# mLSTM outputs of heads 0, 2 and 3 as three products of high and low parts

## The reference

```python
def step(carry, xs):                       # one chunk of 64 steps, all heads at once
    C, n, m = carry
    qc, kc, vc, ic, fc = xs
    b = jnp.cumsum(fc, axis=-1)
    dmat = jnp.where(causal, b[..., :, None] - b[..., None, :] + ic[..., None, :], -jnp.inf)
    inter = b + m[..., None]
    m_row = jnp.maximum(inter, dmat.max(-1))
    w_intra = jnp.exp(dmat - m_row[..., None])
    w_inter = jnp.exp(inter - m_row)
    s = jnp.einsum('bhid,bhjd->bhij', qc, kc) * w_intra
    num = jnp.einsum('bhij,bhjd->bhid', s, vc) + w_inter[..., None] * jnp.einsum('bhvk,bhik->bhiv', C, qc)
    den = s.sum(-1) + w_inter * jnp.einsum('bhk,bhik->bhi', n, qc)
    h = num / jnp.maximum(jnp.abs(den), jnp.exp(-m_row))[..., None]
    ...
mu = hh.mean(-1, keepdims=True)
var = jnp.mean(jnp.square(hh - mu), axis=-1, keepdims=True)
hn = ((hh - mu) * lax.rsqrt(var + LN_EPS)).transpose(0, 2, 1, 3).reshape(B, S, ML_INNER)
hn = hn.astype(h.dtype) * ln_w
return ((hn + skip * x_conv) * jax.nn.silu(z)) @ w_out
```

## Time and profile before

| | |
|---|---|
| median of 3 runs | 1936.8 us |
| profiled execution | 1933.06 us |
| its span | 1931.1 us |
| mean granted clock of TensorE | 0.989 |
| share of the span: TensorE, VectorE, ScalarE, GpSimd | 96%, 57%, 36%, 11% |
| first and last start of the output matmuls (line 1095) | 249.1 and 380.3 us |

### The profile page before, as it was taken

One profiled execution on the slowest core, in us unless ns is written; L12 is line 12 of the kernel. 1 busy time (PEld: TensorE's weight loads), 2 busy tenths in 40 slices (PEclk: granted clock), 3 DMA queues, 4 the chain that ended last, 5 costly groups with the idle time before them and its releaser, 6 DMA issues. The chain is left out here.

```text
span 1931.1 us, 35675 instructions
## 1 busy us (share of the span) xinstructions
PE 1851.7 (96%) x15284; PEld 1484.9 (77%) x15284; DVE 1097.6 (57%) x1648; ACT 693.0 (36%) x1154; POOL 221.5 (11%) x221
## 2 busy tenths in 40 slices
PE   8999999999999899999999899999899999999996
PEld 7887757688887666778888568878878888888875
DVE  4664354563256777444366887777465635354534
ACT  4325332341223787442212473423233322122342
POOL 4210011140002000210021340000001000000011
PEclk9999999999999999999999999999999999999998
DMA  5334323152224010124321100002042322322121
GB/s 187 115 109 142 130 77 116 44 209 99 69 69 141 3 45 2 67 92 141 125 100 55 47 2 4 4 3 69 4 175 90 107 98 90 106 92 105 55 98 44
DMA packets 42379, 160.73 MB, mean 83 GB/s; under 512 B 4976, under 2 KB 14192, under 8 KB 27632
## 3 DMA queue, kind: packets, MB, share of 16 engines
q1 hardware_dynamic: 28016, 143.78, 21.7%
q10 hardware_dynamic: 14208, 14.68, 2.1%
HBM read 140.36 MB, written 16.78 MB: 81 GB/s over the span
## 5 line engine op out<-in xcount | busy, mean ns | idle before, releaser
L257 DVE TENSOR_TENSOR wlo<-raw,whi 128x2048 fp32r<-128x2048 f32 (+2 forms) x113 | 251.4, 2225 | 183.9 <-ACT whi L248 183.6
L248 ACT ACTIVATE whi<-raw 128x2048 fp32r<-128x2048 f32 (+2 forms) x113 | 209.0, 1850 | 317.9 <-PE ps L283 161.4
L281 PE MATMUL ps<-act_hi,whi 128*128 128x512 f32 x616 | 243.6, 395 | 0.0
L301 PE MATMUL ps<-act_lo,whi 128*128 128x512 f32 x632 | 242.0, 392 | 0.0
L283 PE MATMUL ps<-act_hi,wlo 128*128 128x512 f32 x616 | 240.8, 391 | 0.0
L282 PE MATMUL ps<-act_lo,whi 128*128 128x512 f32 x616 | 240.7, 391 | 0.0
L300 PE MATMUL ps<-act_hi,whi 128*128 128x512 f32 x592 | 235.5, 398 | 0.0
L305 PE MATMUL ps<-act_hi,wlo 128*128 128x512 f32 x632 | 156.5, 389 | 0.0
L301 PEld LDWEIGHTS ps<-act_lo,whi 128*128 128x128 f32 x632 | 119.7, 189 | 25.6 <-issue 1.2
L305 PEld LDWEIGHTS ps<-act_hi,wlo 128*128 128x128 f32 x632 | 118.6, 188 | 24.6
L300 PEld LDWEIGHTS ps<-act_hi,whi 128*128 128x128 f32 x592 | 111.1, 188 | 32.2 <-issue 8.1
(11 more groups left out here) (520 smaller groups left out, 3362.0 us busy)
## 6 DMA issues: line engine op xcount, KB each, us to landing
raw<-stream_in SPq DMA_DIRECT2D x107, 1024.0 KB, 4.9
v_scratch<-v_out ACTq DMA_DIRECT2D x16, 256.0 KB, 3.3
z_scratch<-zt ACTq DMA_DIRECT2D x16, 256.0 KB, 2.9
mlh_v<-v_scratch SPq DMA_DIRECT2D x4, 1024.0 KB, 4.8
mlh_z<-z_scratch SPq DMA_DIRECT2D x16, 256.0 KB, 2.6
cmp_w<-cmp_w_in SPq DMA_DIRECT2D x2, 2048.0 KB, 11.3
z_scratch<-in_zt ACTq DMA_DIRECT2D x16, 256.0 KB, 2.2
mix_g<-z_scratch SPq DMA_DIRECT2D x16, 256.0 KB, 6.9
```

The costliest lines, as they stand in the source:

```text
L248: act.activation(k.whi[b % 2][:, 0:n], k.raw[b % RAW_SLOTS][:, 0:n], ACT.Copy).then_inc(k.hi_done, 1)
L257: dve.tensor_tensor(k.wlo[b % 2][:, 0:n], k.raw[b % RAW_SLOTS][:, 0:n], k.whi[b % 2][:, 0:n].bitcast(F32), ALU.subtract).then_inc(k.lo_don ...
L281: pe.matmul(bank, hi, x_hi, start=(x == 0), stop=False)
L301: pe.matmul(bank, hi, x_lo, start=False, stop=False)
```

## The change

Heads 0, 2 and 3 (`SPLIT`) get `split_outputs` in place of `outputs`; head 1 stays as it was. For a split head `v` and `st` are each divided in a high part (`v_hi`, `st_hi`, fp32r copies by ScalarE) and a low part (`v_lo` by GpSimd, `st_lo` by VectorE). A pair (i, j) then is five fp32r matmuls: three of 128x512 and two with two columns of ones (`one`) for the row sum. The parts are laid in places that are used up: `v_lo` in place of `v`, `st_lo` in place of `st`, `st_hi` over the keys whose blocks the scores have read, `v_hi` over `hn` for head 0 and over `xconv` of heads 0 and 1 for heads 2 and 3. The row sums move to every second column of their bank. The line numbers below are those of the kernel before.

```diff
--- before.py
+++ after.py
@@ -962,6 +962,11 @@
     wexp = k.region("mlh_wexp", [P, 2, S], F32, 64)
     z = k.region("mlh_z", [P, 2, S], F32, 68)
     y = k.region("mlh_y", [P, 2, S], F32, 74)
+    SPLIT = [0, 2, 3]
+    v_lo = k.region("mlh_v_lo", [P, TT, S], F32R, 32)
+    v_hi = {h: k.region(f"mlh_v_hi{h}", [P, TT, S], F32R, at) for h, at in zip(SPLIT, (40, 0, 8))}
+    st_hi, st_lo = k.region("mlh_st_hi", [P, TT, S], F32R, 48), k.region("mlh_st_lo", [P, TT, S], F32R, 56)
+    one = k.region("mlh_one", [P, 2], F32R, 72)
     sc = k.small
     den, adn, r, sd, scale, shift = (sc[:, 32 + 4 * i:36 + 4 * i] for i in range(6))
     stats = sc[:, 64:64 + 24].rearrange("p (t s) -> p t s", s=6)
@@ -971,7 +976,7 @@
           "v_landed", "k_mm", "k_act", "k_dve", "nm_mm",
           "sc_mm", "wexp_raw", "wexp_done", "st_done", "h_mm", "hn_done", "hn_dve",
           "tr_mm", "y_read", "y_done", "y_hi", "y_lo", "step", "r2v_done",
-          "sd_done", "scale_done")}
+          "sd_done", "scale_done", "v_hi", "v_lo", "st_hi", "st_lo", "one")}
     zl = [k.sem(f"mlh_z_landed{i}") for i in range(2)]
     LAST = ML_HEADS - 1
 
@@ -985,6 +990,13 @@
 
     def add_bank(n):
         return (4 + n) % 8
+
+    def diagonal(j):
+
+        return st_hi[:, 0:TT - j, j * P:(j + 1) * P]
+
+    def blocks(j):
+        return st[:, j, j * P:S].rearrange("p (i q) -> p i q", q=P)
 
     with k.joined() as block:
         @block.sync
@@ -1034,8 +1046,15 @@
                 pool.tensor_tensor(k.act_lo[:, a, :], y[:, u % 2, :], k.act_hi[:, a, :].bitcast(F32), ALU.subtract) \
                     .then_inc(s["y_lo"], 1)
 
+            def values_low(h):
+                pool.wait_ge(s["v_hi"], SPLIT.index(h) + 1)
+                for j in range(TT):
+                    last = pool.tensor_tensor(v_lo[:, j, :], v[:, j, :], v_hi[h][:, j, :].bitcast(F32), ALU.subtract)
+                last.then_inc(s["v_lo"], 1)
+
             for j in range(TT):
                 triangle(0, j)
+            values_low(0)
             for h in range(ML_HEADS):
                 for c in range(TT):
                     if h < LAST and c == 0:
@@ -1044,6 +1063,8 @@
                         triangle(h + 1, 2)
                     if h < LAST and c == 1:
                         triangle(h + 1, 3)
+                    if c == 2 and h + 1 in SPLIT:
+                        values_low(h + 1)
                     low(h, c)
             norm.gather(pool)
 
@@ -1093,7 +1114,28 @@
                     for j in range(i + 1):
                         lhs = st[:, j, i * P:(i + 1) * P]
                         pe.matmul(k.ps[:, i, :], lhs, v[:, j, :], start=(j == 0), stop=(j == i))
-                        last = pe.matmul(k.ps[:, 7, i:i + 1], lhs, k.const("ones")[:, 0:1], start=(j == 0), stop=(j == i))
+                        last = pe.matmul(k.ps[:, 7, 2 * i:2 * i + 1], lhs, k.const("ones")[:, 0:1], start=(j == 0), stop=(j == i))
+                    last.then_inc(s["h_mm"], 1)
+
+            def split_outputs(h):
+                x = SPLIT.index(h)
+                pe.wait_ge(s["one"], 1)
+                pe.wait_ge(s["v_lo"], x + 1)
+                for i in range(TT):
+                    pe.wait_ge(s["st_lo"], TT * x + i + 1)
+                    if h:
+                        pe.wait_ge(s["y_read"], TT * (h - 1) + i + 1)
+                        pe.wait_ge(s["r2v_done"], h)
+                    if h == 2:
+                        pe.wait_ge(k.evac_done, added(1, 4 + i))
+                    total = k.ps[:, 7, 2 * i:2 * i + 2]
+                    for j in range(i + 1):
+                        hi, lo = st_hi[:, i - j, j * P:(j + 1) * P], st_lo[:, j, i * P:(i + 1) * P]
+                        pe.matmul(k.ps[:, i, :], hi, v_hi[h][:, j, :], start=(j == 0), stop=False)
+                        pe.matmul(k.ps[:, i, :], hi, v_lo[:, j, :], start=False, stop=False)
+                        pe.matmul(total, hi, one[:], start=(j == 0), stop=False)
+                        pe.matmul(k.ps[:, i, :], lo, v_hi[h][:, j, :], start=False, stop=(j == i))
+                        last = pe.matmul(total, lo, one[:], start=False, stop=(j == i))
                     last.then_inc(s["h_mm"], 1)
 
             def turned(h, c):
@@ -1146,7 +1188,7 @@
             for h in range(ML_HEADS):
                 if h < LAST:
                     selected(h + 1)
-                outputs(h)
+                (split_outputs if h in SPLIT else outputs)(h)
                 if h < LAST:
                     keys(h + 1)
                     scores(h + 1, 0)
@@ -1224,11 +1266,30 @@
                 act.wait_ge(s["y_done"], u + 1)
                 act.activation(k.act_hi[:, u % KD, :], y[:, c % 2, :], ACT.Copy).then_inc(s["y_hi"], 1)
 
+            def values_high(h):
+                act.wait_ge(s["v_landed"], 16 * (h + 1))
+                if h:
+                    act.wait_ge(s["y_done"], TT * (h - 1))
+                act.activation(v_hi[h][:], v[:], ACT.Copy).then_inc(s["v_hi"], 1)
+
+            def states_high(h, j):
+                if h in SPLIT:
+                    act.wait_ge(s["st_done"], TT * h + j + 1)
+                    act.activation(diagonal(j), blocks(j), ACT.Copy).then_inc(s["st_hi"], 1)
+
             keys(0, 0)
             keys(0, 2)
+            act.activation(one[:], k.const("ones")[:, 0:2], ACT.Copy).then_inc(s["one"], 1)
             split_hi(k, act, out0 + 1)
-            for j in range(TT):
-                weights(0, j)
+            weights(0, 0)
+            weights(0, 1)
+            values_high(0)
+            states_high(0, 0)
+            weights(0, 2)
+            states_high(0, 1)
+            weights(0, 3)
+            states_high(0, 2)
+            states_high(0, 3)
             for h in range(ML_HEADS):
                 ahead = h < LAST
                 if ahead:
@@ -1241,10 +1302,16 @@
                 normed(h)
                 if ahead:
                     weights(h + 1, 2)
+                    states_high(h + 1, 0)
                 high(h, 0)
                 if ahead:
                     weights(h + 1, 3)
+                    states_high(h + 1, 1)
                 for c in range(1, TT):
+                    if c == 2 and h + 1 in SPLIT:
+                        values_high(h + 1)
+                    if c > 1 and ahead:
+                        states_high(h + 1, c)
                     high(h, c)
                 if h % 2:
                     b = out0 + 4 * (h // 2)
@@ -1290,7 +1357,7 @@
                     then_wait(dve.bn_stats(stats[:, i, :], k.ps[:, i, :]))
                     then_wait(dve.bn_aggr(mv[:, i, :], stats[:, i, :]))
                 floor = k.floor_col[:, :, h]
-                then_wait(dve.tensor_copy(den, k.ps[:, 7, 0:TT]))
+                then_wait(dve.tensor_copy(den, k.ps[:, 7, 0:2 * TT].rearrange("p (t x) -> p t x", x=2)[:, :, 0]))
                 then_wait(dve.scalar_tensor_tensor(out=adn, in0=den, scalar=-1.0, in1=den, op0=ALU.mult, op1=ALU.max))
                 then_wait(dve.tensor_tensor(adn, adn, floor, ALU.max))
                 then_wait(dve.reciprocal(r, adn))
@@ -1325,11 +1392,20 @@
                 dve.wait_ge(zl[c % 2], 16 * (u // 2 + 1))
                 dve.tensor_tensor(y[:, c % 2, :], y[:, c % 2, :], z[:, c % 2, :], ALU.mult).then_inc(s["y_done"], 1)
 
+            def states_low(h, j):
+                if h in SPLIT:
+                    dve.wait_ge(s["st_hi"], TT * SPLIT.index(h) + j + 1)
+                    dve.tensor_tensor(st_lo[:, j, j * P:S].rearrange("p (i q) -> p i q", q=P), blocks(j),
+                                      diagonal(j).bitcast(F32), ALU.subtract).then_inc(s["st_lo"], 1)
+
             keys(0, 1)
             keys(0, 3)
             split_lo(k, dve, out0 + 1)
             for j in range(TT):
                 weighted(0, j)
+                if j:
+                    states_low(0, j - 1)
+            states_low(0, TT - 1)
             for h in range(ML_HEADS):
                 ahead = h < LAST
                 statistics(h)
@@ -1343,6 +1419,8 @@
                     if ahead:
                         weighted(h + 1, c)
                     branch(h, c)
+                    if ahead:
+                        states_low(h + 1, c)
                 if h % 2:
                     b = out0 + 4 * (h // 2)
                     for n in range(KD):
```

## The result

The median after is 1951.09 us (1949.88 to 1952.41), that of before, run beside it, 1937.09 us (1934.7 to 1939.19). The ratio is 1.0075, 95% interval 1.0065 to 1.0086. The direction is the forecast one. The size isn't: +14.0 us where +9.6 was forecast, so the time lies just inside the upper end of the range, in the region of the mutual hold-up, 4.7 us above the forecast.

The account below looks back on a forecast made before the run. TensorE, busy 1851.7 of 1931.1 us, was taken as the bound. Head 0 +4.0 +1.7, head 3 +7.8 +1.7, cheaper pairs -5.6 gave +9.6 us on 1936.8: 1946.4 us, range 1940.5 to 1951.5.

Parts of the forecast that it names:

- mutual hold-up: Rival: GpSimd and VectorE delay each other, standstills 5.3 and 9.8 us, +13.9 us in all, 1950.7 us; chance 0.14.
- The place and the releaser: TensorE idles before the first output matmul of heads 0 and 3, released by GpSimd's `v_lo`; none before head 2.
- the lengths of the standstills: TensorE waits 4.0 us at head 0 (bounds 3.6 to 5.3) and 7.8 us at head 3 (7.2 to 9.8).
- the added instructions beside TensorE: Copies and subtractions on ScalarE, VectorE and GpSimd; at head 2 counted as nothing, up to 1.0 us if VectorE is held.
- would have to begin before 365.5 us: Head 3's `v_lo` subtractions, condition for the rival that parts are ready in time: 1931.2 us, chance 0.05.
- the clock: Behind each new standstill, at heads 0 and 3, half clock makes 1.7 us of work take 3.4: +1.7 us each.
- the two old standstills: Waits of 4.4 us before line 1765 and 4.1 us before line 2236, each followed by granted clock 0.50.
- the pair: In split heads a new pair takes 0.90 us against 1.08; thirty pairs save 5.6 us.
- cheap sums: Rival: two-column sums take the lower bound of the weight load, saving 8.8 us instead of 5.6: 1943.2 us; chance 0.15.
- A sum: Each two-column fp32r sum of a new pair costs 0.11 us, between half of that and 0.23.
- `st_lo` isn't the last: Head 3: VectorE's fourth `st_lo` is done about 377 us, wanted only by the last output row, after 378.4 + 5.4.

Follow-up runs that it names:

- experiment 1: The changed kernel with only head 2 split, heads 0, 1 and 3 keeping the fp32 outputs: 1934.93 us, ratio to before 0.9993.
- experiment 6: The changed kernel with `v_hi` and `v_lo` of the next head made early and rows 0 to 2 adding `v_lo` products last: 1940.99 us, ratio to before 1.0020.
- Experiment 3: The changed kernel with 15 (head 0) or 32 (head 3) unused filler matmuls on TensorE before the `v_lo` wait: 1941.56 us, ratio to before 1.0030.
- 8: The changed kernel with only head 3 split, the other heads keeping the fp32 outputs: 1946.99 us, ratio to before 1.0048.
- 9: experiment 6 with VectorE's order rewritten, some ScalarE and GpSimd steps moved, and low values added after rows 0 and 1: 1935.02 us, ratio to before 0.9994.
- 2: The changed kernel with only heads 0 and 2 split, head 3 as before the change: 1940.22 us, ratio to before 1.0020.
- 5: The changed kernel with `v_hi` and `v_lo` of the next head made earlier on ScalarE and GpSimd, TensorE's order unchanged: 1945.14 us, ratio to before 1.0040.
- experiment 7: The changed kernel with only head 2 split and without the sums over `st_lo`: 1933.0 us in one execution.
- experiment 4: The changed kernel with the `v_lo` products of rows 0 to 2 put behind these rows' other products: 1938.98 us, ratio to before 1.0008.
- 11: 9 with low values added after three rows in heads 0 and 2, two in head 3, and block 1's `st_lo` before weighted block 2: 1936.77 us, ratio 0.9996.

## Why the prediction was short

**Right.** The place and the releaser (`v_lo` of GpSimd, at head 0 and head 3, nothing at head 2); the lengths of the standstills, 3.65 and 7.90 for 4.0 and 7.8; the added instructions beside TensorE cost nothing themselves at head 2 (experiment 1: -1.6 us in the stage with all of head 2's). That the four subtractions of head 3 "would have to begin before 365.5 us" was the right condition for `v_lo`: in experiment 6 they begin at 360.92, and no wait for `v_lo` is left there. It wasn't enough for no loss, since `st_lo` comes next.

**Wrong, the clock.** The step "at half the clock about 3.4 us of work take the place of 1.7" for each standstill. It is the term of the sum that was mis-sized: 5.7 us in place of 3.4, +2.3. The reading of the earlier trace rows holds: the clock's record of before has 3.4 us at half clock behind each of the two old standstills (623.8 to 627.2, 1094.9 to 1098.3). What failed is that their length was carried over to the new ones. Around head 0 the half clock lasts 6.8 us and around head 3 10.2 us, and 5.9 and 6.7 us of that fall on the outputs, where a pair takes 1.71 us in place of 0.92. Experiment 3 gives the same term from outside the account, 5.7 in the pairs. The other half-clock stretches of before, 6.8 us from 842.3 and 10.2 us from 1398.6, had shown that the length varies; I had looked only at the two. It also varies from profile to profile at one and the same standstill. The one of 4.4 us that the earlier trace rows shows has 3.4 us at half clock around it in before, 6.8 in the change, 10.2 in experiments 6 and 8 and 13.7 in 9. Head 0 lost 2.7, 2.5 and 2.4 us to it in the change and in experiments 2 and 5, head 3 3.0 in the change and 1.6 alone. So 1.7 wasn't wrong for every execution of head 3, but it was too small for each of head 0.

**Wrong, a little: the pair.** 0.92 us, not 0.90, and the fast path of the rival "cheap sums" isn't seen for fp32r: loads of 188 to 192 ns at full clock, as in the earlier trace rows. Thirty pairs give back 4.8 and not 5.6 us, +0.8; 0.2 of that is a slip, since 30 x 0.18 is 5.4. A sum is 0.10 to 0.11 us, as estimated (experiment 7); the rest of the 0.02 lies with the products.

**The rival "hold each other up"** gives nearly the measured time, 1950.7, and is still not what happened: its standstills were 5.3 and 9.8, the measured ones are those of the forecast. The hold-up exists, but small. GpSimd's subtractions in the kernel after, all twelve (ns min/median/max):

```profile
L1052 POOL TENSOR_TENSOR mlh_v_lo<-mlh_v,mlh_v_hi x12: 1264/1460/1742, 247.6 to 380.6; 128x512 fp32r<-128x512 f32 x12
```

The median is 0.19 us above an undisturbed one. The four of head 0 take 5.48 us and those of head 3 5.75, which is 0.4 and 0.65 above four undisturbed ones, against the 0.2 and 0.5 that I had allowed. The standstills still agreed because the row before them ran a little earlier (`v_lo` of head 0 begins at 247.56, not 247.8; `v_hi` of head 3 is done 2.0 us behind the scores, not 2.2).

**Blind spot that didn't count here.** "`st_lo` isn't the last" is true, and hid what came next: experiments 5 and 6 fell short on just that, and on the hold-up between GpSimd and VectorE, which the prediction had as a rival and which counts once VectorE is on the path.

**What stays open.** Terms: 9.6, the clock +2.3, the pairs +0.8, the standstills -0.25 and small shifts +0.3 make 12.75, and the stage is at +12.75. The medians differ by 14.0. Across the ten timed experiments and the change the measured difference (ratio times 1937) lies 2 below to 3.4 us above the stage's, 1 above on average, which is about as wide as the intervals, +-2 us. The profiles show one variable thing behind the stage: the time at half clock there (within the span) is 41 us before, 51 after, and 44 to 58 in the experiments. Some 17 us of it are the end of every run; the rest lies, differently in each, at 620 to 650, 840 to 860, 1090 to 1110, 1200 to 1225 and 1340 to 1420 us. A profile with more of it is longer behind the stage: 1549.8 us with 41, 1554.4 with 51 (the change), 1559.0 with 58 (experiment 6).

The mean clocks of the single executions narrow it down, though they are given to three decimals only. The time at half clock is twice the span times what the mean clock lacks to 1. In the 91 executions of the kernel before that were timed beside the experiments it is 47 us on average, from 39 to 58, and an execution with 1 us more of it takes 0.40 us longer. So one and the same kernel differs in this from execution to execution. The profiled one of before has less than most, and so the spans differ by 17.6 us where the medians differ by 14.0. In the six executions of the change it is 68 us, and with the 17 us of the profiled stage taken off, 51. By this estimate the change has some 4 us more at half clock behind the stage, worth about 1.5 us, and 12.75 + 1.5 is near the measured 14.0. Why a change ahead should raise it, no run here tells.

## What to carry to other kernels

On a kernel in which one engine is never idle, a cheaper sequence on it is worth only what its operands leave: find when the last operand can be ready, and take the wait for each operand to its first use, late ones summed last (experiment 4: 13 us of the stage for an edit of TensorE's order alone). Price a standstill of TensorE at its length plus the half clock behind it, with a range for the latter: here it was two thirds to three quarters of the length for the first (2.4 to 2.7 us on 3.65), a fifth to two fifths for the second (1.6 on 8.1, 3.0 on 7.9). And when a wait has been removed, look for the next on the same matmul before forecasting the gain: here it was VectorE's queue, which the earlier work on GpSimd made slower still, and after that TensorE's own order.

## What the runs showed of the hardware

- Short standstills differ in what they bring. Waits of 2.1 and 1.8 us (experiment 4), 1.2 (9) and 1.0 (11) left the clock full, waits of 1.5 us (9, head 0), of 1.0 and 2.1 us (6) and of 0.9 and 1.6 us (5) were followed by 3.4 us at half. The length of the wait alone doesn't decide it, and no run here tells what does.
- The clock can fall during a long standstill: 379 to 382 us is at 0.50 with no matmul at all in it. It fell 0.9 us before work began again at head 0, 3.6 us before at head 3. Behind the waits of 4.4 and 4.1 us in the kernel before and behind the shorter ones of 5, 6 and 9 it fell 0.2 to 1.7 us after work had begun again. It stayed low for 3.4 to 6.7 us of work.
- The half clock isn't twice the time: a pair of outputs took 1.71 us at 1.2 GHz and 0.92 at 2.4.
- A matmul with two columns in fp32r isn't free after a long one: 0.03 us for its own step and some 0.08 more on the next.
- GpSimd's subtraction of 128x512 took 1.26 us at best and up to 1.74 beside VectorE work. VectorE's subtraction of 128x512 took 0.68 us with GpSimd idle (4) and 1.76 beside `v_lo` (6); its difference of two blocks, 128x256, 0.42 us in experiment 6, took 1.49 us in the change while GpSimd worked on `v_lo`:

```profile
377.99 1.49 DVE L1398 TENSOR_TENSOR mlh_st_lo<-mlh_st,mlh_st_hi 128x256 fp32r<-128x256 f32 x1
```
